# Prompt attention: stick chunks scored 18 steps ahead, softmax chunks 20, and the first head's operands loaded ahead of the constants

## What is computed

```python
def stick_breaking_block(q, k, v, q_pos, k_pos):
    z = jnp.einsum('bqhd,bkhd->bhqk', q, k).astype(jnp.float32) * (SB_HEAD_DIM ** -0.5)
    causal = k_pos[None, :] < q_pos[:, None]
    log_beta = jax.nn.log_sigmoid(z)
    log_rem = jnp.where(causal, log_beta - z, 0.0)
    tail = lax.cumsum(log_rem, axis=3, reverse=True) - log_rem
    w = jnp.where(causal, jnp.exp(log_beta + tail), 0.0)
    return jnp.einsum('bhqk,bkhd->bqhd', w.astype(v.dtype), v)

def mla_block(q_nope, q_rope, k_nope, k_rope, v, q_pos, k_pos):
    s = (jnp.einsum('bqhn,bkhn->bhqk', q_nope, k_nope)
         + jnp.einsum('bqhr,bkr->bhqk', q_rope, k_rope)).astype(jnp.float32)
    s = s * ((MLA_NOPE_DIM + MLA_ROPE_DIM) ** -0.5)
    visible = (k_pos[None, :] // CHUNK) <= (q_pos[:, None] // CHUNK)
    s = jnp.where(visible, s, jnp.finfo(jnp.float32).min)
    p = jax.nn.softmax(s, axis=-1)
    return jnp.einsum('bhqk,bkhv->bqhv', p.astype(v.dtype), v)
```

## Time and profile before

| | |
|---|---|
| three executions | 2634.92, 2643.04, 2646.65 us; median 2643.04 |
| the profiled execution | 2648.48 us |
| its span | 2646.7 us |
| busy over the span | PE 2248.5 us (85%), DVE 1381.5 (52%), ACT 1323.5 (50%), POOL 776.9 (29%) |
| prompt attention | from about 1068 us to about 2085 us of the span |
| one head in the middle of it | 122.9 us |
| mean granted TensorE clock | 0.917 |

### The profile page before, as it was taken

How to read it: one execution, slowest core, us unless ns; L and a number is a source line. 1 busy time by engine, 2 the same in 40 slices (tenths; PEclk the granted TensorE clock), 3 DMA queues, 4 the chain that set the end, 5 groups by cost and what they waited for, 6 DMA issues and landing times. The chain is left out here.

```text
span 2646.7 us, 40141 instructions
## 1 busy us (share of the span) xinstructions
PE 2248.5 (85%) x12099; PEld 1869.0 (71%) x12099; DVE 1381.5 (52%) x2759; ACT 1323.5 (50%) x2852; POOL 776.9 (29%) x773
## 2 busy tenths in 40 slices
PE   6599996999977899498989999999989577775887
PEld 1488885899967677286868677777778356664765
DVE  2223232210137333487878778787878388863332
ACT  1223222211112433388888888888888555542221
POOL 0000000000000000356474737465563345542321
PEclk9799998899989899699999999999999777777989
DMA  8333322222337898733323343332320444426773
GB/s 292 106 101 95 108 83 89 100 80 82 116 92 198 284 310 290 158 67 69 68 66 75 70 91 67 68 82 58 74 54 23 107 136 135 142 67 196 177 185 93
DMA packets 304695, 314.44 MB, mean 119 GB/s; under 512 B 88322, under 2 KB 234765, under 8 KB 299489
## 3 DMA queue, kind: packets, MB, share of 16 engines
q1 hardware_dynamic: 299810, 297.45, 40.9%
q10 hardware_dynamic: 3744, 12.19, 1.2%
q0 software_dynamic: 992, 3.21, 0.3%
HBM read 194.83 MB, written 109.57 MB: 115 GB/s over the span
## 5 line engine op out<-in xcount | busy, mean ns | idle before, releaser
L1243 ACT ACTIVATE pa_whi<-banks 128x512 fp32r<-128x512 f32 (+3 forms) x640 | 346.4, 542 | 98.9 <-PE banks L1468 77.9
L1468 PE MATMUL banks<-ident,pa_p 128*128 128x128 f32 x2176 | 354.9, 279 | 2.2 <-ACT pa_p L1208 2.2
L1451 PE MATMUL banks<-pa_khi,pa_qst 128*128 128x512 f32 (+3 forms) x640 | 262.7, 410 | 103.9 <-DVE pa_p L1307 77.1
L1397 POOL TENSOR_TENSOR pa_wlo<-pa_whole,pa_whi 128x512 fp32r<-128x512 f32 (+2 forms) x240 | 279.2, 1172 | 191.4 <-ACT pa_whole L1248 190.7
L1379 POOL CAST pa_khi<-pa_kraw 128x512 fp32r<-128x512 f32 x64 | 39.1, 611 | 993.4 <-DMA pa_kraw<-scratch_sb_kT 993.4
L1468 PEld LDWEIGHTS banks<-ident,pa_p 128*128 128x128 f32 x2176 | 268.5, 143 | 61.4 <-issue 5.6
L1428 PE MATMUL banks<-pa_whi,pa_vst 128*128 128x512 f32 (+3 forms) x640 | 285.1, 445 | 1.5 <-POOL pa_wlo L1397 1.4
L1307 DVE TENSOR_TENSOR_SCAN pa_p<-banks,pa_p,pa_zero 128x512 f32<-128x512 f32 x192 | 246.3, 1283 | 71.4 <-ACT banks L1201 62.6
L1451 PEld LDWEIGHTS banks<-pa_khi,pa_qst 128*128 128x128 f32 x640 | 125.7, 196 | 184.2 <-DVE pa_p L1307 142.7
L1284 DVE TENSOR_TENSOR pa_wlo<-banks,pa_whi 128x512 fp32r<-128x512 f32 (+3 forms) x400 | 234.7, 587 | 27.0 <-ACT pa_whi L1243 27.0
L1452 PE MATMUL banks<-pa_klo,pa_qst 128*128 128x512 f32 (+3 forms) x640 | 242.6, 379 | 0.0
(11 more groups left out here) (231 smaller groups left out, 5095.6 us busy)
## 6 DMA issues: line engine op xcount, KB each, us to landing
ada<-in_ada_w_dram SPq DMA_DIRECT2D x6, 2048.0 KB, 11.4
scratch_sb_kT<-ke_kT SPq DMA_DIRECT2D x12, 1024.0 KB, 8.9
scratch_mla_kT<-ke_nT SPq DMA_DIRECT2D x12, 1024.0 KB, 5.5
scratch_mla_v<-ke_v SPq DMA_DIRECT2D x12, 1024.0 KB, 5.4
co_hlo<-scratch_hT SPq DMA_DIRECT2D x6, 1408.0 KB, 6.9
scratch_gatesT<-co_gates SPq DMA_DIRECT2D x12, 704.0 KB, 10.7
pr_x<-in_x_prompt_dram SPq DMA_DIRECT2D x16, 512.0 KB, 4.4
scratch_hT<-pr_hT SPq DMA_DIRECT2D x16, 512.0 KB, 5.3
```

Of the source, the lines that this page charges most:

```text
L1243: act.activation(whi[:, t % NW, q0:], bank, ACT.Copy).then_inc(hi_done, 1)
L1397: pool.tensor_tensor(wlo[:, t % NW, q0:], whole[:, t % 4, q0:], raw(whi[:, t % NW, q0:]), ALU.subtract).then_inc(pool_lo, 1)
L1451: pe.matmul(bank, qst[job][:, q], khi[job][:, keys], start=True, stop=False)
L1468: y = pe.transpose(ps[:, NS + t % NTB, x * P:(x + 1) * P], probs[g][x][:, i * P:(i + 1) * P], s["ident"][:])
```

## The change

`LEAD` is replaced by `STICK_LEAD` = 18 and `SOFT_LEAD` = 20. Steps 0 to 19 now hold chunks 18 to 37, step 20 holds the two chunks 38 and 39, step 21 the two chunks 40 and 41, steps 22 to 59 hold chunks 42 to 79 as before, steps 60 and 61 hold none, and steps 62 to 79 hold chunks 0 to 17 of the next head. The phase starts with 18 chunks ahead of step 0 instead of 20. The exponentials stay in the steps where they were, and the sigmoids of chunks 0 and 1 move to steps 62 and 63. SP issues keys and queries of head 0 first, then the constants. PE no longer waits for `const_done` at the start but at chunk 40, and it waits for the split keys group by group instead of for all four parts.

```diff
-    LEAD = 20
+    STICK_LEAD, SOFT_LEAD = 18, 20
...
-            return (t + LEAD) % HEAD < JOB and t % 4 != 3
+            return (t + SOFT_LEAD) % HEAD < JOB and t % 4 != 3
...
-        def chunk_at(h, t, last):
-
-            if t + LEAD < HEAD:
-                return h, t + LEAD
-            return (None, 0) if last else (h + 1, t + LEAD - HEAD)
+        def chunks_at(h, t, last):
+
+            grown = JOB - SOFT_LEAD
+            if t < grown:
+                yield h, t + STICK_LEAD
+            elif t < grown + 2:
+                yield h, 2 * t - grown + STICK_LEAD
+                yield h, 2 * t - grown + STICK_LEAD + 1
+            elif t + SOFT_LEAD < HEAD:
+                yield h, t + SOFT_LEAD
+            if t + STICK_LEAD >= HEAD and not last:
+                yield h + 1, t + STICK_LEAD - HEAD
...
-                for job in range(2):
-                    load_k(0, job)
-                    load_q(0, job)
-                    load_v(0, job)
+                load_k(0, 0)
+                load_q(0, 0)
+                sp.dma_start(causal[:], d["const_causal"]).then_inc(const_loaded, 16)
+                sp.dma_start(probs[3][2][:, 0:CH], d["const_own_tile"]).then_inc(kr_loaded, 16)
+                for i in range(3):
+                    sp.dma_start(early[i * ROPE:(i + 1) * ROPE, 0:T], d["mla_krT"][:, 0:T]).then_inc(kr_loaded, 16)
+                load_v(0, 0)
+                load_k(0, 1)
+                load_q(0, 1)
+                load_v(0, 1)
...
-                    chunk(*chunk_at(h, t, last))
-
-                for m in range(LEAD):
+                    for which in chunks_at(h, t, last):
+                        chunk(*which)
+                    for g, i, c in exps_at(t + SOFT_LEAD):
+                        exp(h, g, i, c)
+
+                for m in range(STICK_LEAD):
                     chunk(0, m)
...
-                pe.wait_ge(const_done, 1)
...
+                    if (i, c) == (0, 0):
+
+                        wait_apart(pe, kv_split, kv_upto(h, "k", job) - PARTS + g + 1, passed)
                     if m % JOB == 0:
-                        wait_apart(pe, kv_split, kv_upto(h, "k", job), passed)
                         pe.wait_ge(q_loaded[job], (80 if job else 32) * (h + 1))
+                        if job:
+                            pe.wait_ge(const_done, 1)
```

More of the change, by code:

```diff
@@ L1097, in _ @@
             def _(sp):
-                sp.dma_start(causal[:], d["const_causal"]).then_inc(const_loaded, 16)
-                for i in range(3):
-                    sp.dma_start(early[i * ROPE:(i + 1) * ROPE, 0:T], d["mla_krT"][:, 0:T]).then_inc(kr_loaded, 16)
-                sp.dma_start(probs[3][2][:, 0:CH], d["const_own_tile"]).then_inc(kr_loaded, 16)
                 def load_k(h, job):
```

17 lines of the change are left out of this document (removed).

## The result

| | before | changed kernel |
|---|---|---|
| median, both on one chip, 7 executions each | 2644.38 us | 2656.44 us |
| ratio | | 1.0047, 95% interval 1.0033 to 1.0062 |
| profiled execution, its span | 2648.48, 2646.7 us | 2653.94, 2652.1 us |
| mean granted TensorE clock | 0.917 | 0.919 |

The changed kernel is 12 us slower, by less than the 0.5% that was taken as telling. The prediction was 2650, 7 us above its own value for the kernel before, with a range to 2663. The spans differ by only 5.4 us: in the profiled execution after, the phases ahead of prompt attention were 5.1 us shorter (its first DVE instruction is at 1063.77 us, before at 1068.92) and those behind its last transposes 1.9 us; from this first instruction to the last transposes the changed phase is 12.5 us longer (1024.5 against 1012.1).

What follows compares the result with a forecast made beforehand. No engine is a clean limit; PE leads, so its idle gaps decide. Seven changes of heads at +0.3, eight loops at +0.35 and +0.1, start +1.1: 2643 + 7 = 2650 us, own range 2642 to 2655, 8-in-10 range 2634 to 2663.

Steps and rivals of the forecast that it cites:

- the change of heads: Between heads, seven times: 1.0 us of idling saved, 0.6 carried past chunk 7, outweighed by slow clock; +0.3 us each.
- the stick stretch: Where the ring of two score banks sets the pace: chunks moved to another step keep their place in the ring.
- T 64 starts at 5.37: Change of heads: T 64 comes 5.37 us after T 60, as in the last head of the kernel before.
- I take that it falls: Change of heads: the clock falls behind the new pair of gaps, 3.5 us of idling in some 5 us.
- A spell costs 0.8 us: Price of a stretch at lower clock, from 74.25 us with it and 73.42 without, starting at the short gap.
- T 24 at 10.1: Steps 20 and 21: T 24 comes 10.1 us after T 19, 3.1 later than before.
- Counted at chunks most of that: Steps 20 and 21: most of the delay was already paid as ring places; 0.35 us a head is lost here.
- At the loop's turn, ... about 0.1 us longer: Step 12: chunk 30, 512 wide, replaces chunk 32, 384 wide, so PE's sigmoid wait grows about 0.1 us.
- rival B: Clock stays up at changes of heads: -0.6 each, 2644 us; 2640 if loop's-turn spells go too; chance 0.20.
- 1.1 us slower: The start, once: rotary keys land last of the same bytes, first scan at 1091.1 against 1090.05 us.
- C: Three new PE gaps at steps 20 and 21 lower the clock: 6 to 14 us more, 2656 to 2664; chance 0.20.
- D: Steps 20 and 21 absorb the pairs, changes of heads save 19 us, start up to 6: 2618 to 2624; chance 0.13.

Runs made afterwards that it cites:

- e7: Kernel before with PE's gaps filled by unread matmuls, 18 ahead of chunk 2 and eight at the loop's turn ahead of chunk 34: 2620.89 us, ratio 0.9931.
- e5: Changed kernel with unread matmuls filling PE's gaps at each change of heads, seven ahead of T 64 and five ahead of chunk 2: 2646.36 us, ratio 1.0029.
- e8: Changed kernel with the stick chunks 19 ahead instead of 18: 2666.64 us, ratio 1.0109 to the kernel before.
- e11: e8 with ACT running the exponentials of steps 60 and 61 ahead of the step's sigmoid: 2642.02 us, ratio 0.9998 to the kernel before.
- e3: Changed kernel with DVE keeping the low parts of steps t % 4 = 1 instead of 3: 2645.24 us, ratio 1.0001 to the kernel before.
- e1: Kernel before with only the new order of loads and the finer waits at the start, leads still 20: 2646.59 us, ratio 1.0012.
- e6: Kernel before with 18 unread matmuls filling PE's gap ahead of chunk 2 at each change of heads: 2630.11 us, ratio 0.9961.
- e9: Kernel before with DVE keeping the low parts of steps t % 4 = 1 instead of 3: 2643.51 us, ratio 0.9998.
- e10: e3 and e5 together, with six and five unread matmuls in the two gaps: 2639.01 us, ratio 0.9996 to the kernel before.

## Why the prediction came out as it did

The time, 2656.44, lies 6 us above the 2650 predicted and 1 us above the forecast's own range (2642 to 2655), inside the range given. Against the kernel before the forecast was +7 us and the measurement is +12. The mechanism was right (two smaller gaps, the clock falling behind them, the two chunks given back where DVE is full); two terms of the sum came out too small, the change of heads and the stick stretch, and spells that stayed away at the loop's turn made up for part of it. That part is luck. From the trace, in us, from the phase's first DVE instruction to its last transposes:

| | forecast | measured |
|---|---|---|
| up to T 60 of the first head (the start; steps 20 and 21 once) | +1.5 | +1.1 |
| seven changes of heads, T 60 to chunk 7 | +2.1 | +4.3 |
| seven stick stretches, chunk 7 to chunk 39 | +0.7 | +3.9 |
| chunk 39 to T 24, seven times | +2.5 | +2.1 |
| T 24 of the last head to its last transposes | 0 | +1.1 |
| sum | +6.8 | +12.5 |

The last term is a spell behind T 64 of the last head, which the kernel before doesn't have there.

- **"T 64 starts at 5.37", "chunk 2 starts at 8.0", "two, of about 1.8 and ... 1.7 us"**: 5.52, 8.11, and 1.95 and 1.47. Reading the new order off the last head worked to 0.15 us for the starts and to 0.23 for the gaps. The table load started 5.96 after T 60 (predicted 5.8).
- **"I take that it falls"**: it fell in six of seven. In the one where it didn't, chunk 7 comes 14.89 us after T 60, 0.5 earlier than the 15.42 of before: the gain of 0.6 that was forecast for a clock that stays up is there.
- **"A spell costs 0.8 us"**: right for the loop's turn, from which it was read (0.9 by e7), wrong for the change of heads (1.5 by e7 before, 1.2 to 1.6 after). This is the first term that was too small. The forecast was 0.6 of gain less 0.8, a loss of 0.2 to 0.6 us; with a spell chunk 7 comes 16.12 to 16.53 us after T 60, a loss of 0.7 to 1.1. The Trainium skill, "TensorE: Matmul & The Clock Gate", section "Terms", has the penalty as the time throttled times the share of pulses withheld. By that rule, an estimate, a spell of 3.4 us in the kernel before costs 1.7 us, near the 1.5 measured there and twice the loop's turn; one of 6.8 us in the changed kernel would cost 3.4, and the trace has 1.2 to 1.6. The 2656 worked out by it ahead of the run is the measured median by luck: the rule's price is twice too high for the longer spell, and most of the loss sits in the order of the work.
- **"T 24 at 10.1"**: 10.01, with gaps of 0.65, 0.24 and 0.76 before chunks 39, 40 and 41 (predicted 0.8, 0.4, 0.9). From chunk 39 to T 24 it is 1272.33 - 1266.04 = 6.3 us, as predicted.
- **"Counted at chunks most of that is the place of the two chunks in the ring, which was paid at the start of the stretch before"**: this is the step that failed, and the second term that was too small. It takes the stick stretch to run at one pace whatever stands beside its chunks. From chunk 2 to chunk 39 of the second head the kernel before needs 1268.17 - 1211.49 = 56.68 us, the changed one 1266.04 - 1208.02 = 58.02. It lost 1.3 us, some of it by the spell at its head. With the clock up in both, chunk 7 to chunk 39 takes 48.8 us in e7 and 49.6 to 49.8 in e5: 0.9 us, where the forecast had nothing. That is T 0-12, +1.03 us: each chunk now stands beside the transposes and low part of a step two further on, and PE waits 2.23 us there instead of 1.36. e8 and e11 show how it goes with the lead: 17.03, 17.2 and 18.06 us for leads of 20, 19 and 18. e3 takes 0.4 us of it back by moving DVE's low part. What makes up the other 0.6 was not isolated.
- **"At the loop's turn, ... about 0.1 us longer"**: the gap is 2.4 us instead of 2.0 (why was not isolated), and yet the loop's turn cost less than before, since the spell behind it stayed away in four of six heads (before in one), about 0.9 us each. This was no part of the forecast; rival B had it as an extra. The forecast also counted the 0.1 eight times where such a gap comes in six heads.
- **The start, "1.1 us slower"**: 1.2, and e1 alone 1.2. The rotary keys landed with the same bytes ahead of them; the 1078 end of the range is out, and "the rotary keys land before 1080" reads 17.25 us after the phase's first instruction in the changed kernel, which in the kernel before would be 1086.2, by the row that the prediction went by (1086.05).
- **"+7 us"**: by the table of columns, a head of the new order costs 2.2 us more without any spell, less 0.3 for the cheaper spell at the change of heads and 0.8 where the loop's turn has none. For heads with all of this it is 124.0 - 122.9 = 1.1 us, for heads in which the loop's turn has its spell as before 2.5 (125.4). The seven heads sum to +9.9 us.
- **Rivals.** B was refuted by the clock at the changes of heads and half right at the loop's turn. C's time, from 2656 on, is the measured one and its mechanism isn't: the clock at steps 20 and 21 stays up in all heads (T 19-24 is 10.00 to 10.03 in each). D's 19 us are there in part: e5 shows that with the clock up the change of heads gives 1.9 us from T 60 to T 66 (9.81 against 11.73), but against a kernel before whose clock is up too. The part of its gain that is the clock's at the change of heads can be had without the change: that is e6, 9 us by the medians and 11 inside the phase.

## What to carry to other kernels

Where a ring of buffers sets the pace, shifting a producer by two steps isn't free even if every chunk keeps its place in the ring: here the stretch lost 1.0 us a head. What a chunk stands beside changes (e3 shows 0.4 us of it), so read the pace of the whole stretch for the new pairing, or vary the lead and measure. Closing a wait by moving work pays only where the time at which the work is given back has room; here, with the clock up in both, the change of heads gained 2.0 us up to T 0 of the next head (32.06 against 30.08), 1.0 went in the twelve steps behind it, and 3.0 between T 19 and T 24. A shift can also break the grouping of ACT's functions by table, which, with the clock behind it, cost e8 3.5 us a head and shows only in ACT's rows. Before reordering for the sake of a gap, fill it once with matmuls that nobody reads: it tells what the clock takes, and with both gaps filled was here worth 13.5 us inside the phase and 0.7% by the medians, more than any order tried.

## What the runs showed of the hardware

- The length of a gap doesn't tell whether the clock falls behind it. At the loop's turn of e9 the gap ahead of 1621.45 was 1.82 us and the clock behind it 0.52; in the changed kernel 2.4 us at 1255.63 left it at 1.00 (window above), as did 2.37 us in e5. In the changed kernel itself 2.37 us ahead of 1751.45 was followed by a spell and 2.56 us ahead of 1627.60 was not. The windows behind the gaps of e9 and e5:

```profile
1621.40:1624.90 3.50, 3.45 (x13) 2.86 (x14) 3.11 (x3) 2.73 (x7) 3.42 (x4) 0.52 0.16 37
```

```profile
1496.90:1500.40 3.50, 3.31 (x19) 2.82 (x20) 2.93 (x3) 3.25 (x8) 3.46 (x4) 1.00 0.16 37
```

- How often the clock fell at the loop's turn differs from kernel to kernel: in five of six in the kernel before and in e3, in two in the changed kernel, three in e6, one in e5 and six in e10. The last three have no spell at the changes of heads, some 49 us ahead, so taking spells away at one gap doesn't settle the next. Between these kernels the length of the gap and the time from gap to gap change as well, and each has one profile: what decides was not isolated.
- A spell at half clock of 6.8 us cost 1.2 to 1.6 us and one of 3.4 us cost 1.5 (change of heads) or 0.9 (loop's turn): the price depends on how much of the stretch PE would have waited anyway. At full clock the stretch at 1578.90 has 4.93 us of work for PE in 7.10, room for slower matmuls; the one of e7 at 1203.40 has 6.33 in 6.90. And of the 6.8 us spells the cheaper are those that begin at T 64 and fill the second gap (0.63 us left of 1.47).
- One mean hides this: the mean granted clock was 0.917 before and 0.919 after, with quite different spells; e7 has 0.927.
